# The second part's attentions: negated scores copied to SBUF with their extreme, exponential read from the copy

## What is computed

```python
def gqa_attend(q, k, v):      # 16 query heads of 64, 4 key heads
    s = jnp.einsum('bqhgd,bkhd->bhgqk', q, k).astype(jnp.float32) * (GQA_HEAD_DIM ** -0.5)
    p = jax.nn.softmax(s, axis=-1).astype(v.dtype)
    return jnp.einsum('bhgqk,bkhd->bqhgd', p, v)

def mla_attend(q_nope, q_rope, k_nope, k_rope, v):   # 64 + 32 wide, the rotated 32 shared by all heads
    s = (jnp.einsum('bqhd,bkhd->bhqk', q_nope, k_nope)
         + jnp.einsum('bqhr,bkr->bhqk', q_rope, k_rope)).astype(jnp.float32) * ((MLA_NOPE + MLA_ROPE) ** -0.5)
    p = jax.nn.softmax(s, axis=-1).astype(v.dtype)
    return jnp.einsum('bhqk,bkhd->bqhd', p, v)
```

## Time and profile before

| | |
|---|---|
| runs of the kernel | 1848.34, 1850.47, 1857.23 us, median 1850.47 |
| profiled execution, first to last instruction | 1849.9 us (the page gives this span as its time; the median of the runs is 0.6 above it) |
| mean granted clock of TensorE | 0.990 of full |
| busy: TensorE, its weight loads | 1761.6 us (95%), 968.5 us (52%) |
| busy: VectorE, ScalarE, GpSimd | 748.5 us (40%), 547.8 us (30%), 153.7 us (8%) |
| scores of the grouped-query attention | from 1169.1 to 1328.6 us |
| scores of the latent attention | from 1596.0 to 1781.4 us |
| maxima (L484) of both | 128 instructions, 116.6 us |
| exponentials (L575) of both | 128 instructions, 113.7 us |

### The profile page before, as it was taken

How to read it: one execution, slowest core, us unless ns; L and a number is a source line. 1 busy time by engine, 2 the same in 40 slices (tenths; PEclk the granted TensorE clock), 3 DMA queues, 4 the chain that set the end, 5 groups by cost and what they waited for, 6 DMA issues and landing times. The chain is left out here.

```text
span 1849.9 us, 24504 instructions
## 1 busy us (share of the span) xinstructions
PE 1761.6 (95%) x9830; PEld 968.5 (52%) x9830; DVE 748.5 (40%) x1472; ACT 547.8 (30%) x1119; POOL 153.7 (8%) x194
## 2 busy tenths in 40 slices
PE   8999988999899999999989999999999999999998
PEld 3333455455444444555564444577745644566663
DVE  2244478142511121333233225477624337466642
ACT  2111477123100110333223212345412233344420
POOL 0320001001110110111100014000000002000000
PEclk9999999999999999999999999999999999999999
DMA  7655778447999999999971222000020012000001
GB/s 275 214 210 182 119 151 74 162 163 322 419 416 416 417 416 417 418 417 417 402 287 38 91 91 91 1 1 2 27 80 34 24 40 91 24 1 1 1 24 46
DMA packets 92193, 324.84 MB, mean 176 GB/s; under 512 B 12312, under 2 KB 28824, under 8 KB 65072
## 3 DMA queue, kind: packets, MB, share of 16 engines
q1 hardware_dynamic: 78224, 302.55, 44.9%
q10 hardware_dynamic: 8656, 12.32, 1.9%
q0 software_dynamic: 5200, 8.41, 1.2%
HBM read 317.58 MB, written 14.30 MB: 179 GB/s over the span
## 5 line engine op out<-in xcount | busy, mean ns | idle before, releaser
L1089 PE MATMUL mix_ps<-arena 128*64 128x256 f32 x2048 | 239.7, 387 | 8.9 <-DMA arena<-in_w 4.6
L2176 PE MATMUL tail_ps<-arena 128*128 128x512 f32 x488 | 213.9, 594 | 0.0
L1089 PEld LDWEIGHTS mix_ps<-arena 128*64 128x64 f32 x2048 | 145.7, 139 | 96.5 <-issue 24.9
L977 PE MATMUL mix_ps<-arena,side 128*128 128x512 f32 x384 | 175.8, 610 | 0.7 <-DMA arena<-in_w_in 0.7
L484 DVE TENSOR_REDUCE tail_small<-tail_ps 128x1 f32<-128x768 f32 x128 | 116.6, 952 | 118.9 <-PE tail_ps L351 71.4
L2176 PEld LDWEIGHTS tail_ps<-arena 128*128 128x128 f32 x488 | 92.2, 191 | 110.8 <-issue 110.4
L1101 PE MATMUL mix_ps<-arena 128*64 128x512 f32 x512 | 120.3, 613 | 20.5 <-DMA arena<-in_w 19.9
L977 PEld LDWEIGHTS mix_ps<-arena,side 128*128 128x128 f32 x384 | 72.4, 194 | 102.3 <-issue 84.0
L2176 PE MATMUL tail_ps<-arena,side 128*128 128x512 f32 (+2 forms) x328 | 123.6, 535 | 0.0
L575 ACT ACTIVATE arena<-tail_ps,tail_small 128x768 f32<-128x768 f32 x128 | 113.7, 898 | 4.7 <-DVE tail_small L484 4.7
L370 PE MATMUL tail_ps<-first,arena 128*128 128x128 f32 x768 | 97.9, 277 | 0.4 <-ACT arena L575 0.4
(11 more groups left out here) (405 smaller groups left out, 2341.7 us busy)
## 6 DMA issues: line engine op xcount, KB each, us to landing
arena<-in_w SPq DMA_DIRECT2D x96, 2048.0 KB, 21.2
arena<-in_l_w_mod SPq DMA_DIRECT2D x16, 1024.0 KB, 5.1
arena<-in_l_w_in SPq DMA_DIRECT2D x16, 1024.0 KB, 7.1
arena<-in_w_in SPq DMA_DIRECT2D x12, 1024.0 KB, 9.1
arena<-in_l_w_mod SPq DMA_DIRECT2D x16, 512.0 KB, 4.7
residual<-bias_blocks SPq DMA_DIRECT2D x32, 224.0 KB, 12.3
arena<-in_l_w_in ACTq DMA_DIRECT2D x12, 512.0 KB, 11.1
arena<-in_l_w_out SPq DMA_DIRECT2D x6, 1024.0 KB, 5.2
```

The lines of the kernel that those rows point to most:

```text
L977: last = pe.matmul(ps[:, u % 4], oT[:, k, t * P:(t + 1) * P], weights.slot(W_IN[n, k // 4], 4, 512)[:, k % 4], start=(k == 0), stop=(k == ...
L1089: last = pe.matmul(out[h * CAP:(h + 1) * CAP, 0:H2], x, wb[:, k, h * H2:(h + 1) * H2], start=(k == 0), stop=(k == DK - 1))
L2176: last = pe.matmul(out, lhs(k), rhs(k), start=(k == 0), stop=(k == K - 1))
```

## The change

`Attention` gets a switch, `copied`, which is on for `gqa` and `mla` (and, as before, for the attention with a bias). With it VectorE no longer reduces the scores. It multiplies them by -1, writes them to `pr` in SBUF (`rows_of`, which for `mla` views the row as two halves of 384) and takes their minimum in the same instruction. Before it writes it waits for the transposes of unit n - 2, which read that buffer of `pr`, and no longer for that unit's exponential. ScalarE's exponential reads `pr` with scale -1 and writes it in place, as one row of 768. TensorE's scores wait for `maxed` where they waited for `exped`.

```diff
-                 bias=None, rows_to=None, extra=None, ready=None, spread=None, rotated=None):
+                 bias=None, rows_to=None, extra=None, ready=None, spread=None, rotated=None, copied=False):
...
+        self.copied = copied or bias is not None
...
+    def rows_of(self, n, x):
+        _, _, lo, hi, _, _ = self.units[n]
+        rows = self.mem["pr"][:, n % self.PRB, x, 0:(hi - lo) * P]
+        return rows if self.rotated is None else rows.rearrange("p (c k) -> p c k", c=2)
...
             if n >= LEAD:
-                pe.wait_ge(s["exped"] if self.bias is None else s["maxed"], (n - LEAD + 1) * L)
+                pe.wait_ge(s["maxed"] if self.copied else s["exped"], (n - LEAD + 1) * L)
...
                 dve.wait_ge(s["scored"], n * L + x + 1)
-                if self.bias is None:
+                if not self.copied:
                     if n >= PRB:
                         dve.wait_ge(s["exped"], (n - PRB) * L + x + 1)
-                    dve.tensor_reduce(nm[:, b, x:x + 1], self.scores_of(n, x), AX.X if self.rotated is None else AX.XY, ALU.max, negate=True).then_inc(s["maxed"], 1)
+                    dve.tensor_reduce(nm[:, b, x:x + 1], self.scores_of(n, x), AX.X, ALU.max, negate=True).then_inc(s["maxed"], 1)
+                    continue
+                g, t, lo, hi, _, _ = units[n]
+                if n >= PRB:
+                    last = ("weights", n - PRB, len(self.weight_pieces(n - PRB)) - 1)
+                    dve.wait_ge(s["turned"], ring[last][0] + 1)
+                if self.bias is None:
+                    dve.tensor_scalar(self.rows_of(n, x), self.scores_of(n, x), -1.0, None, ALU.mult, ALU.min,
+                                      accum_out=nm[:, b, x:x + 1]).then_inc(s["maxed"], 1)
                 else:
...
-                in_, scale = (self.scores_of(n, x), 1.0) if self.bias is None else (pr[:, b, x, 0:k], -1.0)
-                to = pr[:, b, x, 0:k] if self.rotated is None else pr[:, b, x, 0:k].rearrange("p (c k) -> p c k", c=2)
-                act.activation(to, in_, ACT.Exp, bias=nm[:, b, x:x + 1], scale=scale,
+                in_, scale = (pr[:, b, x, 0:k], -1.0) if self.copied else (self.scores_of(n, x), 1.0)
+                act.activation(pr[:, b, x, 0:k], in_, ACT.Exp, bias=nm[:, b, x:x + 1], scale=scale,
                                accum_out=sm[:, og_b, z, x:x + 1]).then_inc(s["exped"], 1)
```

More of the change, by code:

```diff
@@ L480, in highest @@
                 dve.wait_ge(s["scored"], n * L + x + 1)
-                if self.bias is None:
+                if not self.copied:
                     if n >= PRB:
                         dve.wait_ge(s["exped"], (n - PRB) * L + x + 1)
-                    dve.tensor_reduce(nm[:, b, x:x + 1], self.scores_of(n, x), AX.X if self.rotated is None else AX.XY, ALU.max, negate=True).then_inc(s["maxed"], 1)
-                else:
[L486 to L489, removed]
+                    dve.tensor_reduce(nm[:, b, x:x + 1], self.scores_of(n, x), AX.X, ALU.max, negate=True).then_inc(s["maxed"], 1)
[7 more added lines that the diff above has]
+                                      accum_out=nm[:, b, x:x + 1]).then_inc(s["maxed"], 1)
+                else:
                     dve.wait_ge(*self.bias["loaded"](g))
@@ L2088, in second_layers @@
                     lambda p, x, kt: proj[:, kt, 256 + (p // 2) * 64:256 + (p // 2 + 1) * 64], 64,
-                    lambda p: gT_x[:, p], gate=True, ready=dict(ring=gqa_ready, scores=gqa_scores, output=gqa_output), spread=1)
+                    lambda p: gT_x[:, p], gate=True, ready=dict(ring=gqa_ready, scores=gqa_scores, output=gqa_output), spread=1, copied=True)
     qn, qr, kn, krT = view(arena, 8192, 2, SEQ), view(arena, 9216, 2, SEQ), view(side_w, 0, 2, AT * P), view(side_w, 1536, AT * P)
@@ L2113, in second_layers @@
                     2, lambda p, x, t, lo, hi: (qn[64 * x:64 * x + 64, p % 2, t * P:(t + 1) * P], kn[64 * x:64 * x + 64, p % 2, lo * P:hi * P]),
-                    lambda p, x, kt: kv[kt][:, 256 * p + P + 64 * x:256 * p + P + 64 * (x + 1)], 64, lambda p: g1T[p], gate=True, ready=dict(ring=mla_ready, scores=mla_scores), spread=2,
+                    lambda p, x, kt: kv[kt][:, 256 * p + P + 64 * x:256 * p + P + 64 * (x + 1)], 64, lambda p: g1T[p], gate=True, ready=dict(ring=mla_ready, scores=mla_scores), spread=2, copied=True,
                     rotated=lambda p, x, t, z: [v[64 * z + 32 * x:64 * z + 32 * x + 32] for v in (qr[:, p % 2, t * P:(t + 1) * P], krT[:, 384 * z:384 * (z + 1)])])
```

## The result

The changed kernel took 1836.27 us (median of 11 runs, 1831.74 to 1849.39) against 1849.66 us of the kernel before (11 runs, 1846.03 to 1857.23). The ratio is 0.9926, 95% interval 0.9907 to 0.9945. I had forecast 1839.7 us, 0.58% faster, in a range from 1836.5 to 1847.5: right in direction and mechanism, within the interval of the ratio in size, but the median lies 0.2 us under the range.

The account below looks back on a forecast made before the run. TensorE was taken to bound the kernel, its scores waiting for ScalarE's exponentials. 9.5 us (short waits and first tiles) + 1.7 (starts) - 0.4 (ends) = 10.8 us off 1850.47 gave 1839.7 us, range 1836.5 to 1847.5.

Parts of the forecast that it names:

- The wait moves from the exponentials to the maxima: TensorE's scores in both attentions: they wait only for the maxima, 0.8 us of cover is left, and the wait vanishes.
- The 22 short waits: TensorE's scores behind an exponential, both attentions: 0.24 us gained at each of 22, 5.3 us.
- The first tiles: Scores at the 14 first tiles of a pair: 0.30 us gained each, between 0.24 and 0.33, together 4.2 us.
- VectorE's operation: Multiply, write and minimum replacing the reduction: a pair costs 1.82 to 2.12 us, taken as 1.95, hidden off TensorE's path.
- ScalarE's exponential: Exponential reading SBUF instead of PSUM: 0 to 0.06 us dearer, taken as 0.03, hidden except at each end.
- The ends: Last tile's transposes waiting for the exponential: 0.2 us lost for each attention, 0.4 in all.
- The starts: Second scores of each attention start earlier: 0.95 us grouped-query, 0.74 latent after a transpose gives back 0.13; together 1.7 us.
- The first tiles were ScalarE's: Forecast's side against the rival that first-tile waits are VectorE's; the rival would save 4.8 us, 1845.7, chance 0.12.
- VectorE as the bound: Rival: the new VectorE operation at half rate makes VectorE the bound, about +20 us, 1870; chance 0.08.
- The fast copy: Rival: VectorE's operation runs at 2x, a pair taking about 1 us, 13.5 us saved, 1837.0; chance 0.04.
- No change: Rival: the 0.24 us per tile reappears as TensorE's waits for transposed-weight banks or slower matmuls, 1850; chance 0.10.

Follow-up runs that it names:

- the last experiments: Changed kernel, each new VectorE operation preceded by a plain copy without minimum of 256 or 512 columns: 1849.53 us (ratio 0.9997) and 1886.30 us (1.0185).
- the repeated comparison: The changed kernel once more, no edit, against the kernel before: 1837.51 us against 1850.04, ratio 0.9936.
- the moved wait: Kernel before, with the first scores' wait for the next pair's copied queries and keys put one tile earlier: 1852.72 us against 1850.81.
- the early transposes: Changed kernel, first half of second pair's queries and keys turned one tile earlier in latent attention: 1837.87 us, again 1837.61; in both attentions 1835.26 us.

## Why the prediction was right and wrong

*The wait moves from the exponentials to the maxima.* Right, with cover of 4.41 - 3.43 = 0.98 us where I had 0.8. The 22 short waits gave 0.25 us each, 5.5 us (5.3 in the sum).

*The first tiles.* I took 0.30 us of at most 0.33 for fear that the two more wait instructions keep their 0.09. They keep nothing once nothing is waited for: 0.34 us each, 4.8 us in place of 4.2.

*VectorE's operation.* I took 1.95 us for two, inside 1.82 to 2.12. The second starts 0.88 or 0.89 us behind the first and lasts 0.955, so two take 1.84, at the low end: the masked form of the earlier trace rows was the right neighbour and the read-out of 0.08 us overlaps wholly. Each start so gave more than forecast (1.11 and 1.02 us for 0.95 and 0.87) and the transpose behind them gave back 0.03 us of 0.13: 2.1 us in place of 1.7. The plain TENSOR_SCALAR of the last experiments, without a minimum, took 422 ns for 256 columns and 689 for 512, 1.04 ns an element, so the minimum isn't what keeps the operation from a faster form. On the page of the Trainium skill that I weighed (VectorE: DVE Perf Modes), these traces agree with the section on PSUM operands, fp32 from PSUM at 1x, and not with the 2x that the tier table leaves open for `tensor_scalar`.

*ScalarE's exponential.* 927 ns from SBUF against 898 from PSUM, the 0.03 us that I took, and hidden. The ends lost 0.08 us each, not 0.2, since the minima were hardly later. The same page of the Trainium skill, in its section on the TRN2 errata, gives ScalarE 224 cycles from SBUF and 172 from PSUM, 43 ns apart at its 1.2 GHz, an estimate from the page; the rows show 29 ns, and they decide.

*The sum.* 5.5 + 4.8 + 2.1 - 0.2 = 12.2 us by the terms as measured and 12.1 by the stretches, against 10.8. All four terms erred to the same side.

*The failed step.* The mechanism held, and what failed is the size of the sum, first of all its term for the 14 first tiles: 4.2 us forecast, 4.8 measured, because I left 0.04 us each to the two wait instructions that in the end cost nothing. The starts follow (1.7 forecast, 2.1 measured), then the short waits and the ends (0.2 each). Of the 3.4 us between the forecast 1839.7 and the measured 1836.27 these terms make 1.3, the start from the median of three runs (1850.47, of eleven 1849.66) 0.8, and scatter of the medians 1.3. The range was drawn too tight for this as well. Its fast end, 1836.5, came from a rival that was itself unlikely and not from the bounds of the forecast together with the scatter of medians. I subtracted from 1850.47, a median of three, and said that it lay 0.6 us above the span. In the runs after, the time lies 1.7 to 1.9 us above the span (1840.27 for the span of 1838.5), so the profiled execution before had by that taken about 1851.7, above their median; and the median of 11 runs was 1849.66. With 12.1 us the mechanism gives 1837.6 from 1849.66, and the repeated comparison gave 12.5 us in place of 13.4. A range reaching 3 us past the high bound of the gain (11.5) would have held it.

*The rivals.* The first tiles were ScalarE's (shown by the moved wait). VectorE as the bound is real, but begins to cost at about 1.1 us a step (the estimate above), and the operation has 0.88. The fast copy doesn't exist here. No change: the time didn't reappear elsewhere, 262.46 us between the attentions in both kernels.

## What to carry to other kernels

When PSUM is the buffer that an engine's next work waits for, let whoever reads it first, and has time, carry it out to SBUF in the same pass: here the copy cost VectorE nothing over the reduction (955 against 952 ns), took two exponentials of 0.9 us out of the cycle, and gave TensorE back 0.34 or 0.25 us a tile. Cost the cover on the carrying engine at its densest tile, not at the usual one. And take a forecast's size from start-to-start distances, which for the same stretch at the same granted clock repeated within 0.1 us here, but its range from the scatter of whole runs, which in the traces here lies mostly in another part of the program.

## What was unexpected of the hardware

*A multiplication, a write to SBUF and a minimum cost what the reduction cost:* 955 ns for 768 float32 columns from PSUM against 952, and the read-out of 83 ns overlaps the next operation.

*The low clock.* After TensorE idled 1.9 to 3.4 us ahead of the second scores of the latent attention, the work that followed ran in part at the 1.2 GHz level in 8 of 9 traces, at 1.3 to 1.7 us of loss in most; after idling 0.9 us in none of three. At the start of the grouped-query attention, behind 1.9 us of idling, it fell in 3 of 12. Whether the shorter idle time is the reason was not isolated, since the same three traces also hold the early transposes; and the trace of the kernel before, with 2.95 us of idling, has no such fall. The change is not the reason either: the kernel with only the first wait moved and the one with only the grouped-query attention copying have the fall with the old waits in the latent attention.
